# A recurrent layer that stores the split halves of its weights in DRAM once and loads them back, in place of splitting the raw weights in every quarter

## The reference

```python
h = rmsnorm(x, norm_w)
xb, gb = jnp.split(h @ w_in, 2, axis=-1)
gate = jax.nn.gelu(gb, approximate=True)
xc = conv_b + xp[:, 0:seq] * conv_w[0]              # xp is xb padded by 3 in front
for tap in range(1, LRU_CONV_W):
    xc = xc + xp[:, tap:tap + seq] * conv_w[tap]
xr = xc.reshape(bsz, seq, LRU_BLOCKS, LRU_BLOCK_W)
r = sigmoid(einsum('bsni,nij->bsnj', xr, w_rgate) + b_rgate)
i = sigmoid(einsum('bsni,nij->bsnj', xr, w_igate) + b_igate)
log_a = -LRU_C * r * softplus(-lam)
a, mult = exp(log_a), sqrt(-expm1(2.0 * log_a))
hs = scan over time of  h = a * h + xc * i * mult
y = hs * gate
return y @ w_out
```

## Time and profile before

| what | value |
|---|---|
| median of 3 runs | 3324.17 us (3321.96 to 3325.31) |
| profiled execution, its own time | 3325.53 us |
| its span in the profile | 3324.0 us, 46214 instructions |
| mean granted TensorE clock | 0.905 |
| busy over the span | PE 81%, DVE 57%, ACT 45%, POOL 21% |
| lru in the trace | from 1767.7 us (first load) to 2332.2 us (last y made) |

### The profile page before, as it was taken

One profiled execution on the slowest core, in us unless ns is written; L12 is line 12 of the kernel. 1 busy time (PEld: TensorE's weight loads), 2 busy tenths in 40 slices (PEclk: granted clock), 3 DMA queues, 4 the chain that ended last, 5 costly groups with the idle time before them and its releaser, 6 DMA issues. The chain is left out here.

```text
span 3324.0 us, 46214 instructions
## 1 busy us (share of the span) xinstructions
PE 2699.6 (81%) x12218; PEld 2149.8 (65%) x12219; DVE 1897.1 (57%) x3349; ACT 1505.0 (45%) x2058; POOL 706.0 (21%) x458
## 2 busy tenths in 40 slices
PE   4999969999699577988883999998799378999840
PEld 3777747777587466766762877776577356777630
DVE  3444434444366567456554788876466687544745
ACT  3444544455344244444443676675344344444423
POOL 0000000000011245344441010000011354344532
PEclk8999979999899789999996999999899698999975
DMA  3122212222444287777757455431543487777757
GB/s 109 64 70 70 76 63 70 70 76 76 151 146 132 87 284 272 266 256 259 263 197 235 147 181 161 144 120 51 191 136 126 160 294 278 263 264 252 265 205 256
DMA packets 360028, 563.86 MB, mean 170 GB/s; under 512 B 30608, under 2 KB 272416, under 8 KB 359968
## 3 DMA queue, kind: packets, MB, share of 16 engines
q1 hardware_dynamic: 314080, 402.11, 37.1%
q0 software_dynamic: 29616, 101.76, 9.1%
q10 hardware_dynamic: 16272, 59.25, 4.4%
HBM read 427.77 MB, written 135.30 MB: 169 GB/s over the span
## 5 line engine op out<-in xcount | busy, mean ns | idle before, releaser
L1285 POOL TENSOR_TENSOR experts_gu_lo<-experts_gu_raw,experts_gu_hi x64 | 385.6, 6025 | 160.5 <-ACT experts_gu_hi L1309 159.9
L118 PE MATMUL experts_ps<-experts_gu_hi,experts_hT_hi 128*128 (+1 forms) x760 | 331.8, 437 | 91.4 <-issue 71.3
L119 PE MATMUL experts_ps<-experts_gu_lo,experts_hT_hi 128*128 (+1 forms) x760 | 319.7, 421 | 0.0
L120 PE MATMUL experts_ps<-experts_gu_hi,experts_hT_lo 128*128 (+1 forms) x760 | 318.0, 418 | 0.0
L1366 DVE TENSOR_TENSOR experts_gu_lo<-experts_gu_raw,experts_gu_hi (+1 forms) x64 | 279.7, 4371 | 67.0 <-ACT experts_gu_hi L1309 67.0
L1309 ACT ACTIVATE experts_gu_hi<-experts_gu_raw (+1 forms) x128 | 238.0, 1908 | 91.3 <-DMA experts_gu_raw<-in_moe_w_up 32.1
L118 PE MATMUL route_ps<-route_w_hi,route_src_hi 128*128 128x512 f32 x512 | 215.1, 420 | 56.8 <-DVE route_w_lo L979 56.8
L118 PEld LDWEIGHTS experts_ps<-experts_gu_hi,experts_hT_hi 128*128 128x128 f32 x760 | 156.1, 205 | 141.0 <-issue 106.9
L118 PE MATMUL gla_ps<-gla_wvg_hi,gla_hT_hi 128*128 128x512 f32 x512 | 212.6, 415 | 0.0
L120 PE MATMUL route_ps<-route_w_hi,route_src_lo 128*128 128x512 f32 x512 | 208.7, 408 | 0.0
L119 PE MATMUL route_ps<-route_w_lo,route_src_hi 128*128 128x512 f32 x512 | 208.6, 407 | 0.0
(11 more groups left out here) (311 smaller groups left out, 6571.4 us busy)
## 6 DMA issues: line engine op xcount, KB each, us to landing
experts_gu_raw<-in_moe_w_gate SPq DMA_DIRECT2D x64, 1024.0 KB, 5.7
experts_gu_raw<-in_moe_w_up SPq DMA_DIRECT2D x64, 1024.0 KB, 10.8
experts_wd_raw<-in_moe_w_down SPq DMA_DIRECT2D x64, 1024.0 KB
y_rows<-experts_y ACTq DMA_DIRECT2D x97, 512.0 KB, 6.3
gla_w_raw<-in_gla_w_in SPq DMA_DIRECT2D x18, 1024.0 KB
y_rows<-gla_zeros POOLq DMA_DIRECT2D x8, 2048.0 KB, 8.4
route_src<-oT_rows SPq DMA_DIRECT2D x32, 512.0 KB, 4.3
x_rows<-route_x_new SPq DMA_DIRECT2D x32, 512.0 KB, 2.9
```

Of the source, the lines that this page charges most:

```text
L118: nc.tensor.matmul(out, w_hi, x_hi, start=first, stop=False)
L119: nc.tensor.matmul(out, w_hi, x_lo, start=False, stop=False)
L120: return nc.tensor.matmul(out, w_lo, x_hi, start=False, stop=last)
L1285: pool.tensor_tensor(gu_lo[:, slot(e), DVE_SHARE:], gu_raw[:, slot(e), DVE_SHARE:], gu_hi[:, slot(e), DVE_SHARE:].bitcast(F32), ALU.subtract)\
```

## The change

In the first quarter (steps 0 to 3) the weights are loaded raw and split as before, and SP also stores both halves of each kind in DRAM (`keep`). From step 4 on nothing is split. SP loads both halves straight into hi and lo (`reload`), and PE waits for these loads in place of the low half. The hi and lo buffers are single as before, so a reload of step n + 1 waits until PE has used the weights of step n (`used`), and a split of step n + 1 waits until the stores of step n have read theirs (`kept`).

```diff
+            def keep(kind, n):
+                after(sp, kind["lo_done"], n)
+                for c, part in enumerate(("hi", "lo")):
+                    sp.dma_start(kind["store"][c, n], kind[part][:].bitcast(F32)).then_inc(kind["kept"], DMA)
+
+            def reload(kind, n):
+                after(sp, kind["used"], n - 1)
+                after_dma(sp, kind["kept"], 2 * (n % LRU_BLOCKS) + 1)
+                for c, part in enumerate(("hi", "lo")):
+                    sp.dma_start(kind[part][:].bitcast(F32), kind["store"][c, n % LRU_BLOCKS]).then_inc(kind["loaded"], DMA)
+
+            def next_weights(kind, n):
+                if n + 1 < LRU_BLOCKS:
+                    keep(kind, n + 1)
+                    if n + 2 < LRU_BLOCKS:
+                        load(kind, n + 2)
+                elif n + 1 < STEPS:
+                    reload(kind, n + 1)
...
-            after(sp, wx["lo_done"], 0)
+            keep(wx, 0)
             load(wx, 1)
...
                 for kind in (wx, wg):
-                    if n + 2 < STEPS:
-                        after(sp, kind["lo_done"], n + 1)
-                        load(kind, n + 2)
+                    next_weights(kind, n)
                 if n + GT + 1 < NT:
                     store_x(n + GT + 1)
-                if n + 2 < STEPS:
-                    after(sp, wr["lo_done"], n + 1)
-                    load(wr, n + 2)
+                next_weights(wr, n)
...
             def split(kind, n):
                 after_dma(act, kind["landed"], 2 * n + 1 if kind is wr else n)
+                after(act, kind["used"], n - 1)
+                after_dma(act, kind["kept"], 2 * n - 1)
...
-                if n + 1 < STEPS:
+                if n + 1 < LRU_BLOCKS:
                     split(wx, n + 1)
...
+            def weights(kind, n):
+                if n < LRU_BLOCKS:
+                    after(pe, kind["lo_done"], n)
+                else:
+                    after_dma(pe, kind["loaded"], 2 * (n - LRU_BLOCKS) + 1)
+
             def branch(kind, n, bank, done):
                 q = n // LRU_BLOCKS
-                after(pe, kind["lo_done"], n)
+                weights(kind, n)
...
+    halves = {name: scratch(f"{name}_halves", shape) for name, shape in (
+        ("wx", [2, LRU_BLOCKS, P, KD, LBW]), ("wg", [2, LRU_BLOCKS, P, KD, LBW]),
+        ("wr", [2, LRU_BLOCKS, P, 2, LCT, LBW]))}
```

More of the change, by code:

```diff
@@ L1497, in vector, with lru @@
                                        in1=x[:, j], op0=ALU.mult, op1=ALU.add).then_inc(self.x_done, 1)
-def lru(nc, k, x_dram, y_rows, x_out, norm_w, w_in, conv_w, conv_b, w_r, b_r, w_i, b_i, lam, yT_dram):
+def lru(nc, k, x_dram, y_rows, x_out, norm_w, w_in, conv_w, conv_b, w_r, b_r, w_i, b_i, lam, yT_dram, halves):
     STEPS = NT // GT * LRU_BLOCKS
@@ L1519, in lru @@
                               lo=m.sb(name + "_lo", shape, F32R), landed=m.plain(name + "_in"),
-                              hi_done=m.plain(name + "_hi_done"), lo_done=m.plain(name + "_lo_done")))
+                              hi_done=m.plain(name + "_hi_done"), lo_done=m.plain(name + "_lo_done"),
+                              kept=m.plain(name + "_kept"), loaded=m.plain(name + "_loaded"),
+                              store=halves[name]))
         wx, wg, wr = kinds
@@ L1550, in lru @@
         order = m.plain("vector_order")
+        for kind, used in ((wx, xb_ps_done), (wg, gb_ps_done), (wr, rg_ps_done)):
+            kind["used"] = used
         block = m.block()
@@ L1611, in _ @@
                 next_x(t + 2)
-            after(sp, wx["lo_done"], 0)
+            keep(wx, 0)
             load(wx, 1)
-            after(sp, wg["lo_done"], 0)
+            keep(wg, 0)
             load(wg, 1)
-            after(sp, wr["lo_done"], 0)
+            keep(wr, 0)
             load(wr, 1)
@@ L1892, in gates @@
             def gates(n):
-                after(pe, wr["lo_done"], n)
+                weights(wr, n)
                 after(pe, xc_lo_done, n)
@@ L2007, in build @@
         lru(nc, k, x1, y_rows, x2, lru_norm[0], lru_w_in[0], lru_conv_w[0], lru_conv_b[0],
-            lru_w_rgate[0], lru_b_rgate[0], lru_w_igate[0], lru_b_igate[0], lru_lambda[0], oT)
+            lru_w_rgate[0], lru_b_rgate[0], lru_w_igate[0], lru_b_igate[0], lru_lambda[0], oT, halves)
         project_and_route(nc, k, "route1", oT, lru_w_out[0], x2, x3, h_rows, moe_norm[1],
```

## The result

The kernel became slower: 3406.89 us, the median of 4 runs (3403.15 to 3411.51) against 3324.74 (3321.96 to 3326.78), a ratio of 1.025 with a 95% interval of 1.0234 to 1.0266. The forecast was 3384 in a range of 3352 to 3412, so 23 us too little and only 5 us inside the upper end. The profiled execution took 3403.15 us (span 3401.6), 77.6 us more than the one before.

A forecast was written before the change was run, and what follows sets the result against it. The loop through ACT and DVE sets the 31.3 us step, PE nearly full; afterwards wx's reload: 11.45 + 14.03 + 8.5 = 34.0. Delays 36.0 + 1.0 + 22.8 (clock) = 59.8 on 3325.5 give 3385.3, median 3384, range 3352 to 3412 us.

The forecast's parts named there:

- The mechanism: In stage lru, wx's reload behind y lands last, so PE idles before branch(wx); a step takes 34.0 us without clock falls.
- the first quarter costs nothing: Steps 0 to 2: added stores taken as 0, at most 12 us; rival of choked mixed traffic 3396 us, 10%.
- some 5: Sign in the profile: PE waits some 5 us before branch(wx) in 12 steps, released by a DMA of wx.
- every 34 to 36.5: Sign in the profile: from step 4 on take_xb comes every 34 to 36.5 us.
- The rival that ended on the other side: SP's reload of wx behind y is hidden, wg's split leaves the root chain: 19 us less, 3305 us; chance 6%.
- The break-even at y + 5.8: Reload of wx landing 5.8 us after y ends gives today's 31.3 us step; a single 1 MB load would just make it.
- take_xb to the end of y: From take_xb(n) to y of n - 1 (convolution, norm of a tile, recurrence): 14.03 us a step.
- 36.0 + 22.8: Delay of take_xb(15): 36.0 us from eleven steps of 34.0 without clock falls, plus 12 x 1.9 = 22.8 for the clock.
- the landing: From y to both wx halves landed: 0.4 + 5.3 + 2.6 + 0.3 = 8.6, taken as 8.5 us; bounds 7.7 and 11.8.
- the clock: PE's clock falls in each new gap before branch(wx): 1.9 us each, bounds 0 and 2.5; rival without falls 3361 us, 12%.
- The tail: Behind take_xb(15): stays, but gates(15) end about 1 us later for ACT, +1.0 us.
- The row at 4.29 us: PE's one 4.29 us gap in the kernel before: twelve slow matmuls behind it, 2.4 us, taken as nearest to the new gaps.

The follow-up runs named there:

- experiment 3: Changed kernel, but wx loaded raw and split in all steps, never stored; only wg and wr reloaded: 3307.4 us, ratio 0.9947 to the kernel before.
- experiment 2: Changed kernel with the first quarter's stores of the halves kept, but no reloads; all 16 steps split raw weights: 3325.86 us, ratio 1.0002 to the kernel before.
- Experiment 1: Changed kernel with the reload of wx issued at the top of SP's step, without the wait for y: 3306.4 us, ratio 0.9942 to the kernel before.
- experiment 7: Kernel before, no stores or reloads, with ACT's split of wg moved ahead of take_gate: 3302.49 us, ratio 0.9943.
- experiment 4: Changed kernel reloading only the high half of wx from step 4 on: 3365.65 us, ratio 1.012 to the kernel before.
- experiment 5: Changed kernel with the reload of wx issued in front of the store of y, still behind the wait for y: 3384.57 us, ratio 1.0187 to the kernel before.
- experiment 8: Changed kernel with the halves of wx and wg in DRAM in rows of 1 KB, not 8 KB: 3408.39 us, ratio 1.0264 to the kernel before.

## Why the prediction was right, and where its sizes were off

**The mechanism.** Right, point by point. The reload of wx stands behind y, PE waits for it in 12 of 12 steps and for no other reload, take_xb is released by PE and not by the root, wg and wr are in time (experiment 3 too), and the first quarter costs nothing (take_xb(3) at 1927.47, where it was at 1927.16; experiment 2). Experiments 1 and 3 each remove the lateness of wx in another way and arrive at the same 3306 to 3307. The signs came out larger than they were forecast: PE's wait was 5.9 to 7.8 us and not "some 5", and take_xb came every 37.3 to 38.3 us from step 4 on, not every 34 to 36.5.

**The rival that ended on the other side** was priced at 3305 with steps of 29.7 and 28.3 us. Experiment 1 makes it true by moving the issue: 3306.4, 29.85 and (in the last quarter, take_xb at 2227.29 and 2255.54) 28.25. Its reason, the 1.92 us of wg's split on ACT's chain, is shown by experiment 7. The break-even at y + 5.8 fits as well: in experiment 4 PE starts mostly some 7 us after y, and the kernel is still slower than before.

**The terms of the sum.**

| term, each of 12 steps | predicted | measured |
|---|---|---|
| y to branch(wx) | 8.5 us | 9.74 us |
| branch(wx) to take_xb, with the clock | 11.45 + 1.9 | 13.84 (11.45 + 2.4) |
| take_xb to the end of y | 14.03 us | 14.06 us (2040.98 to 2055.04) |

Take_xb(15) came at 2378.66, 79.95 us later than before, where the prediction had 36.0 + 22.8 = 58.8. The difference of 21 us is 12 x 1.24 for the landing and 12 x 0.5 for the clock. The tail was 0.4 us longer, not 1.0, and the stages behind lru were 2.7 us shorter in this execution (3401.6 - 2412.5 against 3324.0 - 2332.2). That leaves 17.8, which is 77.6 - 59.8.

*The landing* is the term that was mis-sized, and in it what the store of y in front does: 0.4 of issue and 0.3 of delay in the sum. The loads themselves were not too cheap. Before the last four pairs of wx in experiment 1 SP issues nothing for 4 us, and nothing behind them for 13 us (its DMA issues of 2165 to 2260 us):

```profile
lru_wx_hi<-wx_halves SPq DMA_DIRECT2D x4, 1024.0 KB, 4.9
lru_wx_lo<-wx_halves SPq DMA_DIRECT2D x4, 1024.0 KB, 7.0
```

The low half is issued 0.37 us behind the high one, so a pair alone takes 7.4 us from its first issue to its last landing, less than the 5.3 + 2.6 of the sum. With the store of y right in front the median is 9.0: so for wx in the changed kernel, where wg queues right behind, and so for wg in experiment 1, where in the first eight steps nothing follows for 10 us. So what queues behind adds nothing there, and the store in front holds the pair back by 1.5 us, not 0.3. Gathered rows are not the difference: there are none in steps 13 to 15 of the changed kernel, and their pairs take 8.7 to 9.5. With its issue (0.5) the store makes it some 9.5 us from y, the median of the 12 steps; a few late pairs bring the mean to 9.75. With nothing in front and the store and wg right behind (experiment 5) a pair takes 8.4 us, so neighbours behind cost 1.0 us there, and experiment 5 measures only the difference. The store itself lands 3.5 to 3.8 us after its issue with the reloads behind it, and 2.8 in the kernel before. By what mechanism neighbours in the queue hold each other back stays open; the rows' length is not it (experiment 8).

The rule of the Trainium skill ("DMA: Bandwidth & Descriptors", the anatomy of one DMA), 2.0 us plus bytes at 436 GB/s, would have 6.8 us for the two loads (an estimate by the page). The page has fitted it on DMAs that GpSimd issues, which the prediction leaves out; these are issued by SP. The trace has 7.4 us for the pair alone and 8.95 in the changed kernel. The measurement decides.

*The clock* fell to its 1.2 GHz level in every one of the 12 gaps of 5.9 to 7.8 us, as expected, and each fall cost 2.4 us (2.0 to 2.7) by the profile. I had taken a value between those of the shorter gap (1.6) and of the longer one (2.4). The row at 4.29 us would have given the right size, but by luck: there the granted clock was 0.50 from 1786 to 1827 us, so it did not fall in that gap. Nor does the length of the gap set the price: in experiment 8 the gaps are longer (6.4 to 7.5 us) and a fall costs 1.7. What counts is how much of the low stretch is left when the matmuls resume. In the changed kernel the clock fell 1.5 us before branch(wx, 7) began and stayed low for the first 5.3 us of it; in experiment 8 it fell 3.1 us before the same branch and stayed low for 3.7 us of it. The Trainium skill ("TensorE: Matmul & The Clock Gate", the section on HAM oscillation) says that a matmul loop which waits for data in each pass gets throttled anew in each; the trace agrees, 12 of 12; with the shorter gaps of experiment 4 (2.9 to 5.1 us) it was 10 of 12.

## What to carry to other kernels

Work that is moved from engines to a DMA trades a step of slack for a landing time. Ask where the issue stands in its queue, what wait stands in front of it there, and what of the buffer's single copy it must wait for; here one wait that had nothing to do with wx cost 100 us. Before removing work, find which part of it is on the chain: of the splits, some 5 us a step on ACT (1.9 + 1.9 + 1.0) and 6 on DVE (2.3 + 2.3 + 1.2), only the 1.92 us of wg's on ACT lay on the chain (1.5 of them came back), and one instruction moved into an idle stretch gave all of the gain with no traffic. And an idle gap of PE that grows has a second price, the clock, which comes on top as soon as the matmuls behind it are on the path.

## What the runs showed of the hardware

- A gap of 5.9 to 7.8 us before a run of 48 matmuls brought the clock to its 1.2 GHz level each time (12 of 12), and cost 2.4 us in the mean; gaps of 6.4 to 7.5 us in experiment 8 (12 of 12) cost 1.7. Of the gaps of about 2.1 us in the kernel before four in seven did, at 1.6 us each; those of 0.7 us never did. Filler matmuls of 0.23 us in the gap kept it at 1.00 over 240 us.
- Two loads of 1 MB, issued 0.4 us apart, land 7.4 us after the first issue when alone in the queue, 9.0 with a 0.5 MB store right in front, and 8.4 with the store and 2 MB more right behind.
- With the DMA engines full, loads with rows of 8 KB moved at 414 to 418 GB/s, with rows of 1 KB at 348 to 351.
- Behind many DMAs in a row an issue itself can take long. In the prologue of the changed kernel, with 3 MB issued in the 2.1 us before, the next issue took 4.54 us, and one a few MB later 9.01, in place of some 0.4 (timeline of SP's queue; the DMA engines were full then, and no run here tests the cause):

```profile
1818.85 4.54 SPq L1592 DMA_DIRECT2D wg_halves<-lru_wg_hi  x1
...
1826.48 9.01 SPq L1592 DMA_DIRECT2D wr_halves<-lru_wr_hi  x1
```

Nothing on the path stood behind them here (take_xb(3) came as early as before), but whatever stands behind such an issue in SP's stream waits for it.
